# One Hymba block on one core: where x comes back, who takes low parts, and the order around two norms

## The reference

```python
h = rms_norm(x, ln1_g);  p = h @ w_in                       # one projection for both head groups
o_rwkv = rwkv7_bidirectional(...)                           # scan in both directions, per-head norm, gate
o_att  = windowed_gqa_alibi(q, ka, va, sink)                # banded attention, 8 query heads
x = x + jnp.concatenate([o_rwkv, o_att], axis=-1) @ w_out   # output projection
h = rms_norm(x, ln2_g)
gate = depthwise_conv_centred(h @ w_gate, conv_w, conv_b)   # width 3 along the tokens
x = x + (gelu(gate) * (h @ w_up)) @ w_down                  # d_ff = 2816
return rms_norm(x, lnf_g)
```

## Time and profile before

| | us |
|---|---|
| time, median of 3 runs | 1383.38 (1381.33 to 1386.67) |
| the profiled execution | 1386.02 |
| its span, first to last instruction | 1384.2 |
| TensorE matmuls busy | 1280.6 (93%) |
| VectorE busy | 858.5 (62%) |
| ScalarE busy | 521.6 (38%) |
| POOL busy | 234.7 (17%) |

### The profile page before, as it was taken

How to read it: one execution, slowest core, us unless ns; L and a number is a source line. 1 busy time by engine, 2 the same in 40 slices (tenths; PEclk the granted TensorE clock), 3 DMA queues, 4 the chain that set the end, 5 groups by cost and what they waited for, 6 DMA issues and landing times.

```text
span 1384.2 us, 28323 instructions
## 1 busy us (share of the span) xinstructions
PE 1280.6 (93%) x11272; PEld 1001.0 (72%) x11272; DVE 858.5 (62%) x1093; ACT 521.6 (38%) x729; POOL 234.7 (17%) x244
## 2 busy tenths in 40 slices
PE   6999999887589988899999999999999989999996
PEld 2476776776456656578778888888888878888875
DVE  4987686799557778773397565555565554333335
ACT  3735345221256667731234333333333331112220
POOL 1001001021312233500006212222222110000000
PEclk9999999998689999899999999999999999999998
DMA  5037768796767777414103332223232373222203
GB/s 212 20 97 182 184 154 184 189 274 155 186 185 235 236 227 221 135 45 144 69 31 92 91 91 77 69 81 91 91 91 65 118 270 136 94 91 72 57 23 122
DMA packets 145830, 179.53 MB, mean 130 GB/s; under 512 B 52432, under 2 KB 107792, under 8 KB 145776
## 3 DMA queue, kind: packets, MB, share of 16 engines
q1 hardware_dynamic: 136384, 152.16, 36.9%
q0 software_dynamic: 4288, 12.98, 3.5%
q10 hardware_dynamic: 5104, 13.67, 3.1%
HBM read 121.16 MB, written 57.54 MB: 129 GB/s over the span
## 4 chain that ended last, share of the span: by engine, by line
PE 73%; DVE 13%; DMA 6%; issue 3%; SPq 2%; ACT 2%; POOL 1%; DVEq 0%; ACTq 0%; POOLq 0%
PE banks L1106 28%; PE banks L694 17%; PE banks L676 6%; PE banks L1143 5%; PE banks L682 3%; DVE work L1966 2%; DVE work L1970 2%; PE banks L1080 2%; DMA work<-in_w_in 2%; PE banks L658 2%; PE banks L884 1%; PE banks L974 1%; PE banks L900 1%; PE banks L1088 1%; PE banks L923 1%
## 5 line engine op out<-in xcount | busy, mean ns | idle before, releaser
L1106 PE MATMUL banks<-op,sw_hi 128*128 128x512 f32 x1120 | 344.6, 389 | 0.0
L1106 PEld LDWEIGHTS banks<-op,sw_hi 128*128 128x128 f32 x1120 | 210.3, 188 | 43.6
L1106 PE MATMUL banks<-op,sw_lo 128*128 128x512 f32 x560 | 217.8, 389 | 0.0
L2152 DVE TENSOR_TENSOR xT<-xT,banks 128x1024 f32<-128x1024 f32 x23 | 28.1, 1220 | 157.7 <-PE banks L694 145.9
L1106 PEld LDWEIGHTS banks<-op,sw_lo 128*128 128x128 f32 x560 | 105.1, 188 | 21.7
L1470 ACT ACTIVATE sw_hi<-work 128x1024 fp32r<-128x1024 f32 (+1 forms) x60 | 72.1, 1204 | 112.2 <-PE banks L1106 109.1
L1762 DVE TENSOR_TENSOR sw_lo<-work,sw_hi 128x1024 fp32r<-128x1024 f32 (+1 forms) x60 | 84.3, 1406 | 37.2 <-ACT sw_hi L1470 37.2
L676 PE MATMUL banks<-ph_hi,pw_hi 128*128 128x512 f32 x272 | 88.1, 406 | 8.3 <-DVE pw_lo L1762 3.8
L1736 POOL TENSOR_TENSOR work<-work 128x512 f32<-128x512 f32 x20 | 28.7, 1435 | 378.6 <-DMA work<-in_w_gu 246.5
L676 PE MATMUL banks<-ph_hi,pw_lo 128*128 128x512 f32 x272 | 86.0, 398 | 0.0
L694 PE MATMUL banks<-g_hi,down_hi 128*128 128x512 f32 x256 | 79.8, 393 | 4.5 <-DVE g_lo L1762 4.0
(11 more groups left out here) (276 smaller groups left out, 2493.3 us busy)
## 6 DMA issues: line engine op xcount, KB each, us to landing
work<-scan_d SPq DMA_DIRECT2D x32, 768.0 KB, 5.0
work<-in_w_gu SPq DMA_DIRECT2D x88, 256.0 KB, 4.6
scan_d<-work SPq DMA_DIRECT2D x16, 1024.0 KB, 5.4
g_d<-hT SPq DMA_DIRECT2D x22, 512.0 KB, 2.9
scan_d<-work SPq DMA_DIRECT2D x32, 256.0 KB, 6.6
work<-in_w_down SPq DMA_DIRECT2D x16, 512.0 KB, 3.7
work<-in_w_in ACTq DMA_DIRECT2D x15, 512.0 KB, 4.0
work<-g_d SPq DMA_DIRECT2D x15, 512.0 KB, 4.5
```

The source lines that it names most:

```text
L1106: mm = pe.matmul(banks[:, 3 * slot + bank, :], w[:, n, k * P:(k + 1) * P], x[n][:, k, :], start=(opens and k == 0 and p_ == 0), stop=(k == ...
L2152: tt(x, x, product, ALU.add).then_inc(added[slot], 1)
```

## The change

Four places change. (1) All low parts of the attention rows 4 to 7 are made on VectorE (`attention_lo`), POOL's two are gone, and `weights_lo(0, 0)` goes ahead of the y sums. The new order there is: w_lo(0), y sums, rows 4 and 5, both variances, rows 6 and 7, w_lo(1), the y normalisings. (2) The copies sw_hi 2 and 3 and their low parts stand between the first half's root (reciprocal) and the second's. (3) `split_g(4)` on VectorE goes ahead of the last pair's convolution. x tiles 0 and 1 count on a semaphore of their own, first_back; VectorE waits for it ahead of the first addition of the down projection, and for the other six ahead of the third. (4) The last token sums are made in two rounds into the same PSUM column: first of acc without the last tile's squares, then of those squares themselves (sqb[1]); VectorE no longer adds the last squares to acc, and `add_square_half(1, m - 1)` stands ahead of `add_half(1, m)`.

```diff
+        first_back = sem("first_back")
...
-            token_norm(4 * (KD - 1), range(4, NT))
+            for source, ready, count in ((acc, ns["summed"], 4 * (KD - 1) - 1), (sqb[1], ns["squared"], 4 * KD)):
+                pe.wait_ge(ready, count)
+                for t in range(4, NT):
+                    mm = pe.matmul(token_sums[:, t:t + 1], source[:, t * P:(t + 1) * P], ones[:, 0:1],
+                                   start=(source is acc and t == 4), stop=(source is not acc), skip_group_check=True)
+            mm.then_inc(ns["ms_mm"], 1)
             spread(3, range(4, NT))
...
-            act.activation(sw_hi[:, 2, :], wsrc[0][:, 3], ACT.Copy)
-            act.activation(sw_hi[:, 3, :], wsrc[0][:, 6], ACT.Copy).then_inc(fs["w_hi"], 1)
+                if h == 0:
+                    act.activation(sw_hi[:, 2, :], wsrc[0][:, 3], ACT.Copy)
+                    act.activation(sw_hi[:, 3, :], wsrc[0][:, 6], ACT.Copy).then_inc(fs["w_hi"], 1)
...
             pool.wait_ge(ys_stored[0], 64 * NC // 4 + FREE)
-            for k in (4, 7):
-                pool.wait_ge(sp_s["att_hi"], KD + k - NPAIR + 1)
-                pool.tensor_tensor(h_lo[:, k, :], oT[:, k, :], h_hi[:, k, :].bitcast(F32), ALU.subtract)\
-                    .then_inc(sp_s["att_lo"], 1)
...
-                pool.dma_start(xT[:, k, :], x_d[k]).then_inc(s["x_again"], 16)
+                pool.dma_start(xT[:, k, :], x_d[k]).then_inc(first_back if k < 2 else s["x_again"], 16)
...
+            weights_lo(0, 0)
             for b in range(2):
                 y_sum(NT - 2 + b, NT // 2, b)
                 y_mean(NT - 2 + b, NT // 2, b)
                 y_centre(NT - 2 + b, b)
-            weights_lo(0, 0)
+
+            def attention_lo(k, done):
+
+                low_part(h_lo[:, k, :], oT[:, k, :], h_hi[:, k, :], sp_s["att_hi"], KD + k - NPAIR + 1, done)
+
+            attention_lo(4, sp_s["att_lo"])
+            attention_lo(5, sp_s["o_lo"])
             y_variance(NT - 2, 0)
-            low_part(h_lo[:, 5, :], oT[:, 5, :], h_hi[:, 5, :], sp_s["att_hi"], KD + 2, sp_s["o_lo"])
             y_variance(NT - 1, 1)
+            attention_lo(6, sp_s["o_lo"])
+            attention_lo(7, sp_s["att_lo"])
             weights_lo(1, 0)
-            low_part(h_lo[:, 6, :], oT[:, 6, :], h_hi[:, 6, :], sp_s["att_hi"], KD + 3, sp_s["o_lo"])
...
-            first_pair_lo(2, 3)
-            first_pair_lo(3, 6).then_inc(fs["w_lo"], 1)
+                if h == 0:
+                    first_pair_lo(2, 3)
+                    first_pair_lo(3, 6).then_inc(fs["w_lo"], 1)
...
             up_first(LAST_F, 1)
+            split_g(4)
             convolve(LAST_F, 1)
-            split_g(4)
             split_g(5)
...
-            dve.wait_ge(s["x_again"], 2 * 16 * KD)
             for gi in range(len(GROUPS) - 1):
                 for i in range(KD // 2):
                     for slot in range(2):
+                        if gi == 0 and i == 0:
+                            dve.wait_ge(first_back, 16 * 2)
+                        elif gi == 0 and i == 1:
+                            dve.wait_ge(s["x_again"], 16 * (2 * KD - 2))
                         add_product(down_unit(gi), i, slot)
...
             for m in range(KD):
-                add_half(1, m)
                 if m >= 2:
                     add_square_half(1, m - 1)
+                add_half(1, m)
                 if m == 2:
                     rstd(2, slice(0, 4))
                 if m >= 3:
                     normalised_half(0, range(2 * m - 6, 2 * m - 4) if m < 7 else ())
-            add_square_half(1, KD - 1)
```

## The result

| | before | after |
|---|---|---|
| time, median | 1387.56 us (1381.33 to 1393.28, 10 runs) | 1376.85 us (1371.27 to 1381.39, 10 runs) |
| the profiled execution | 1386.02 | 1381.39 |
| its span, mean granted clock | 1384.2, 0.969 | 1379.4, 0.962 |

The ratio of the times is 0.9925, with a 95% interval from 0.9903 to 0.9946: 10.4 us less, from 7.5 to 13.5. The forecast was 10.05 less. The time itself, 1376.85, lies inside the range and 3.55 above the forecast, and the median of before came out 4.2 higher in this comparison than in the three runs shown at first.

What follows compares the result with a forecast made beforehand. TensorE was taken as the bound, with time to gain only at four seams: 1.7 + 0.7 + 6.3 + 1.35 = 10.05 us, taking the median from 1383.38 to 1373.3; range 1370.0 to 1378.3.

Steps and rivals of the forecast that it cites:

- Rival (d): End of the scan: VectorE is the bound, two turns lost and ScalarE late; gain 0 there, time 1375.0; chance 0.08.
- rival (a): Down projection: eighth g tile stays late, TensorE stops over 2 us, clock falls; gain there 2.6, time 1377.0; chance 0.15.
- Rival (b): Last norm: the clock stays up in the tail, 0.9 us more gain, time 1372.4; chance 0.16.
- Rival (c): Gate/up products lose pace, each of 20 pairs waiting; slower than before, 1387 us at 0.7 us a pair; chance 0.03.

Runs made afterwards that it cites:

- e11: Kernel before with g tile 4 split ahead of the convolution and x awaited in two portions, nothing else; ratio 0.9954 (0.9932 to 0.9976).
- e12: Changed kernel with the g tile 4 split back behind the convolution and all x awaited at once; ratio 0.9991 (0.9968 to 1.0013).
- e6: Kernel before with x awaited in two portions (first_back) alone, g tile 4 still split behind the convolution; 1381.82 us, one run.
- e2: Kernel before with split_g(4) ahead of the last convolution alone, all x still awaited at once; ratio 1.0006 (0.9985 to 1.0028).
- e4: e3 with four narrow throwaway sums (eight one-column matmuls) on TensorE ahead of the last sums; 1377.98 us, one run.
- e8: Changed kernel with 512-column throwaway matmuls around the second norm, nine ahead of the sums and five between the spreads; 1382.02 us, one run.
- e9: Changed kernel with e7's order, e8's wide throwaway matmuls and five more wide ones in the last norm; ratio 0.9919 (0.9898 to 0.9939), median 1373.69 us.
- e5: Changed kernel with VectorE waiting for all eight x tiles ahead of its first down-projection addition; 1385.09 us, one run.
- e1: Kernel before with all four low parts on VectorE and w_lo(0) ahead of the y sums, nothing else; 1393.06 us, one run.
- e3: Changed kernel with the last token sums in one round again, behind VectorE's last square sum; 1375.62 us, one run.
- e7: Changed kernel with w_lo(0) behind the y sums again and w_lo(1) behind the y normalisings; 1373.88 us, one run.
- e10: The kernel of e7 again, timed: w_lo(0) and w_lo(1) late in the changed kernel; ratio 0.9918 (0.9894 to 0.9942), median 1373.87 us.

## Why the prediction was right, step by step

**The total.** 10.05 forecast, 10.4 measured (7.5 to 13.5). Time can be assigned to part 3 by runs of its own (6.4 us alone, 3.3 to 9.4, e11); for the other three the marks of the executions are the evidence, and their sum in timed runs, 1.2 us (-1.8 to 4.4, e12), does not contradict the 3.75 forecast and does not show it. The changed kernel stands 4.0 us below e11 by the ratios, with intervals that overlap. Part 2 was not run alone.

**Part 1, right in its places, against an end before the change that is not one number.** The list on VectorE went as worked out: the first y sum ended 6.46 behind the softmax scaling, 0.98 later than before where 1.15 was forecast; the first product came at 11.65 (forecast 11.72), the transposes at 20.05 (forecast 20.07). The turns between POOL and VectorE are as read from the earlier trace rows: w_lo(0) at 585.07 and the y sum at 586.28, which took 1.54, lie beside POOL's 3.06 for two instructions. The half clock that the prediction put on the first pair did not come (0.70), and that cost or gave nothing, since the transposes wait for the last y normalising. What the prediction did not weigh is that the turns of before can fall out otherwise. With the old order the transposes came at 21.78 to 21.81 in three executions (before, e6, e11), where POOL's low part of row 7 started ahead of VectorE's of row 6, and at 20.45 in one (e2), where it started behind it. So the gain is 1.7 against the first and 0.4 against the second. In e2 the high parts came 0.64 later, behind an attention product; why that product was late is open. Rival (d), gain 0 because VectorE would be the bound, fell: VectorE is the bound, but sooner (y normalised at 19.99 against 20.54).

**Part 2, right.** Mark B with the old order is 6.89 to 8.52 in five executions, median 8.08; with the new one and no wide matmuls 6.08 to 7.89 in seven, median 7.21. Slowest against slowest that is 0.6, fastest against fastest 0.8, forecast 0.7. The scatter is TensorE's clock during the sixteen sums, which took from 1.92 us at full clock to 3.54. Take their length off mark B and nearly all scatter is gone: 4.97 or 4.98 is left in the five executions of the old order, 4.34 to 4.36 in six of the new, and 4.16 or 4.17 in the three of the new whose sums took 1.92 (e4, e8, e9). So the part gives 0.6 behind slow sums and 0.8 behind fast ones. In the profiled pair mark B fell by 1.25, since the sums were faster as well, and half of that was lost again, since the products behind the norm ran slow for longer (mark C 45.75 against 45.09).

**Part 3, right in its sum, wrong inside.** Mark D fell by 6.30, forecast 6.3. The g tile came as said: a flight of 5.1 us where 4.5 was taken, its low part ended at 1133.93, and TensorE began the eighth tile's products at once; rival (a) did not happen, though with a margin near nothing. The step that failed is "they come 4.9 us sooner, but output tile 2 is due 6.3 us sooner, and without the split into two semaphores 1.4 us would come back here". The x loads left 4.3 us sooner (e2) and landed 0.3 us sooner, because the last one's flight grew from 11.04 to 15.00 (14.97 in e5). What held the landing is not shown beyond that. Without the split 7.7 us come back, stop and half clock behind it (e5), and the swap alone is worth nothing (e2). The two stops of before stood one behind the other and covered for each other: the 4.04 before the eighth g tile hid that x would be 5.7 us late. Taking away the first alone moves the wait; taking away the second alone leaves the first (e6, stop 2.25 with a short flight of the g load, mark D 2.4 above the changed kernel's); both together give 6.3, or 6.3 to 8.0 against the three executions of the old order (561.37, e12 562.28, e1 563.07; in the last two the last x load flew 12.61 and 13.12). The forecast of the sum survived because the split was part of the change, so that no term rested on the landing of the late x tiles.

**Part 4, right, and more in the profiled pair by chance of the clock.** The first spread came 0.6 sooner, its wait 0.87 instead of 1.47, and 0.56 is what it gives on mark E (e6 against e3), 0.6 forecast. Two rounds against one give 0.7 (e3 against e5, e7, e8, e12), 0.75 forecast. Together, with the last spread slow on both sides and the sums of the last squares at about 1.05, mark E fell from 74.74 (e6) to 73.46 to 73.48, that is 1.3; with the spread fast on both sides from 73.91 (e11) to 72.56, 1.35. Forecast 1.35. The profiled pair shows 2.54, because its last spread took 1.16 instead of 2.08, and its last sums 1.05 instead of 1.35.

**Rival (b), the clock in the tail.** It came true in the profiled execution after, and is not borne out as a mechanism. With one-column sums in the pause the last spread took 1.16 once (after), 1.74 once (e10) and 2.07 five times (e4, e5, e7, e8, e12); with the pause unfilled it took 1.16 once too (e11) and 2.04 to 2.08 five times (before, e1, e2, e3, e6). The Trainium skill's rule (TensorE: Matmul & The Clock Gate, Part 1: The HAM clock gate), that the rate follows how busy TensorE has been lately, applied to such sums as the prediction weighed it, would have made the spread of e4 as fast, and there the measurement decides against it. Behind the wide matmuls of e8 and e9 the sums, and in e9 the spread, ran fast, as by the rule; but they did so in other executions without them (sums in e2 and e4, spread in after and e11), so that these two do not show it.

**Rival (c).** The link of the gate/up products is 380.80 or 380.81 us in all fourteen profiled executions: the loop kept its pace.

**Open.** What sets the start of the softmax scaling, and which executions get the half clock at the end of the scan, in the second norm and in the tail. The shift in the profiled pair is there well before the change, at a VectorE copy at 543.85 before and 549.49 after. No run here tells whether the order of the scan's transfers does it.

## What to carry to other kernels

Stops that stand one behind the other cover for each other: before pricing the removal of the first, ask of the second what it would be if its work came no sooner at all, and test each alone. A transfer that left sooner among others did not land sooner here (up to 4.3 us earlier out, the same landing to 0.6); take the old landing time as one bound of the new. And compare a seam in several executions, slow clock with slow and fast with fast, since a microsecond of a small edit is less than what the clock, or which of two engines comes first, gives or takes there.

## What the runs showed of the hardware

- A DMA load of the same 512 KB took 3.4 to 10.5 us on the line of g, and the last of the x loads 11.04, 12.61 (e12), 13.12 (e1), 14.97 (e5) and 15.00 us (e2), longer where it was issued sooner; in the changed kernel the eight x loads took 5.1 to 17.4, while the DMA engines were 0.85 busy at 313 GB/s.
- A VectorE low part of 1.22 us took 2.72 and 3.40 beside a POOL instruction that started first, and 1.21 where it started 0.06 ahead of one (e2); then the VectorE instruction behind it took 2.65 instead of 0.69.
- Behind a pause with 0.95 us of one-column matmuls in it the spread took 2.07 (e4), behind one with five wide ones 1.08 (e9, one execution). The sums of the second norm took 1.92 behind nine wide ones (e8, e9), and without them 1.92 twice (e2, e4) and 2.49 to 3.54 in ten executions.
- The same code at the same place ran at either clock: in kernels with two rounds of last sums and no wide matmuls in the tail the last spread took 1.16 once, 1.74 once and 2.07 four times. The transposes of e7's kernel came at 18.04 and at 20.37, by when TensorE's attention products came.
- Between executions of a one-core kernel a point 42% into the span moved by 9.6 us (572.26 to 581.82), more than most of the edits are worth.
